# One layer's expert-routing head in another order of work (Trainium2, one core)

## The reference, cut to what matters

```python
x = x + gt1 * (mix @ w_out)
h2 = _rmsnorm(x, n2) * (1 + sc2) + sh2
# _peer(h2):
q = (hf @ wq).reshape(n, PEER_HEADS, 2, PEER_QUERY_DIM // 2)
s = jnp.einsum('nhpd,hpkd->nhpk', q, subkeys)
sv, si = lax.top_k(s, PEER_TOPK)                 # 16 of 128 keys, per half and head
cand = sv[:, :, 0, :, None] + sv[:, :, 1, None, :]
top_v, top_pos = lax.top_k(cand, PEER_TOPK)      # 16 experts per head
gates = jax.nn.softmax(top_v, axis=-1)
act = gelu(einsum('td,tkd->tk', xb, u[eb]))
y = einsum('tk,tkd->td', gb * act, v[eb])
```

## Time and profile before

| | us |
|---|---|
| median of 3 runs | 4270.94 (4268.42 to 4283.64) |
| the profiled execution, own time | 4267.19 |
| its span, first to last instruction | 4265.4 |
| PE busy | 3870.5 (91%) |
| DVE busy | 2707.2 (63%) |
| POOL busy | 1624.6 (38%) |
| ACT busy | 688.1 (16%) |

### The profile page before, as it was taken

How to read it: one execution, slowest core, us unless ns; L and a number is a source line. 1 busy time by engine, 2 the same in 40 slices (tenths; PEclk the granted TensorE clock), 3 DMA queues, 4 the chain that set the end, 5 groups by cost and what they waited for, 6 DMA issues and landing times. The chain is left out here.

```text
span 4265.4 us, 40162 instructions
## 1 busy us (share of the span) xinstructions
PE 3870.5 (91%) x13798; PEld 2277.4 (53%) x13798; DVE 2707.2 (63%) x6039; ACT 688.1 (16%) x1538; POOL 1624.6 (38%) x1498
## 2 busy tenths in 40 slices
PE   1699878889999999999879998688999999999997
PEld 1467657655555555554335675666555555555543
DVE  5855278996666666767522732989876565565443
ACT  1031225530000000000011312455100000000000
POOL 0020005545655654545401100355376565454330
PEclk9896789999999999999989859899999999999998
DMA  6400202368999999999830111133799999999874
GB/s 224 137 14 28 109 15 104 141 221 308 380 381 373 377 370 387 366 382 372 325 137 2 41 40 74 50 126 146 256 389 402 400 361 358 368 349 348 334 277 147
DMA packets 359004, 1025.92 MB, mean 241 GB/s; under 512 B 30225, under 2 KB 131857, under 8 KB 355089
## 3 DMA queue, kind: packets, MB, share of 16 engines
q0 software_dynamic: 147456, 536.94, 32.9%
q1 hardware_dynamic: 205810, 428.62, 27.8%
q10 hardware_dynamic: 5536, 57.80, 3.3%
HBM read 964.02 MB, written 59.22 MB: 240 GB/s over the span
## 5 line engine op out<-in xcount | busy, mean ns | idle before, releaser
L1726 PE MATMUL ps<-colsT,arena 128*128 128x384 f32 x4096 | 1364.3, 487 | 9.5 <-DMA arena<-in_peer_ut 9.5
L1726 PEld LDWEIGHTS ps<-colsT,arena 128*128 128x128 f32 x4096 | 777.3, 191 | 588.1 <-issue 98.5
L1761 PE MATMUL ps<-arena 128*128 128x512 f32 x1536 | 676.5, 592 | 0.0
L1261 POOL DMA_INDIRECT proj<-in_peer_u,eidx x336 | 446.3, 1328 | 255.4 <-DVE modbc L1448 130.5
L1247 POOL TENSOR_SCALAR x<-iota,modbc 128x128 f32<-128x128 f32 x192 | 156.1, 829 | 930.7 <-ACT modbc L1576 787.3
L1261 POOL DMA_INDIRECT proj<-in_peer_v,eidx x335 | 360.7, 1077 | 344.1 <-DVE colsT L1459 243.5
L1761 PEld LDWEIGHTS ps<-arena 128*128 128x128 f32 x1536 | 291.7, 190 | 345.5 <-issue 317.7
L1448 DVE CUSTOM_DVE_ANT_0 proj<-proj,rows 128x1024 f32<-128x1024 f32 x336 | 401.3, 1222 | 77.2 <-DMA proj<-in_peer_u,eidx 75.8
L1459 DVE SCALAR_TENSOR_TENSOR colsT<-proj,modbc,colsT 128x1024 f32<-128x1024 f32 x330 | 409.0, 1285 | 4.2 <-DMA proj<-in_peer_v,eidx 4.1
L1761 PE MATMUL ps<-arena,rows 128*128 128x512 f32 x768 | 344.7, 601 | 13.9 <-DMA arena<-in_peer_v 13.9
L1761 PE MATMUL ps<-arena,x 128*128 128x512 f32 x768 | 341.6, 597 | 7.2 <-DMA arena<-in_peer_v 7.2
(11 more groups left out here) (284 smaller groups left out, 4307.4 us busy)
## 6 DMA issues: line engine op xcount, KB each, us to landing
arena<-in_peer_ut SPq DMA_DIRECT2D x256, 512.0 KB, 7.0
arena<-in_peer_v SPq DMA_DIRECT2D x256, 512.0 KB, 7.0
gmat_d<-arena ACTq DMA_DIRECT2D x24, 2048.0 KB, 6.5
arena<-gmat_d SPq DMA_DIRECT2D x64, 768.0 KB, 18.1
modbc<-in_w_adaT SPq DMA_DIRECT2D x48, 512.0 KB, 4.1
proj<-in_w_adaT SPq DMA_DIRECT2D x48, 512.0 KB, 9.1
arena<-in_w_out SPq DMA_DIRECT2D x2, 4096.0 KB, 14.2
arena<-in_w_q SPq DMA_DIRECT2D x2, 4096.0 KB, 20.8
```

Of the source, the lines that this page charges most:

```text
L1261: pool.indirect_dma_start(ring[slots[at]], None, tab, bass.IndirectOffsetOnAxis(ap=eidx[:, b * SLOTS + q:b * SLOTS + q + 1], axis=0)).then ...
L1726: mm = pe.matmul(ps[:, 2 + j % 2, 0:ND], utab[:, j % UR, k], hT[:, k, NG:T], start=(k == 0), stop=(k == KT - 1))
L1761: mm = pe.matmul(ps[:, Y_BANKS[2 * d + c2], :], wT[j % CR][:, d * P:(d + 1) * P], vtab[:, j % VR, c2 * 512:(c2 + 1) * 512], start=(j == 0) ...
```

## The change

All of it is in the head, in both layers. The amount of arithmetic is the same.

- Query units 0 to 5 are now one block and four heads each: 0 and 1 block 2, 2 and 3 block 3, 4 and 5 block 4. PE does the queries and scores of block 2 before the rows of block 3 are turned.
- The third and fourth output projection are made in halves with other PE work between; PSUM banks change (OP_BANKS, TR_BANKS).
- On ACT the root is a call of its own after the square.
- On DVE, residual, mean and normalisation of the blocks stand at other steps of `route(0)`; those of block 1 (i = 4) move into k = 1: mean after step 0, normalisation after step 1.
- Queries 4 and 5, which stood before the loop over k, are fillers of k = 1; query 9 moves to k = 2; the scores of blocks 4, 0 and 1 stand at (1, 3), (2, 1) and (2, 6).
- The 18 u slices: none in k = 1, 7 in k = 2, 11 in k = 3.
- The turned indices (ijgT) lie in another free row of modbc, and the indirect loads' ring takes its slots in an order that fits this.

```diff
-        QUNITS = ([(2, 2, 2 * i, 2, i) for i in range(4)] + [(4, 1, 4 * i, 4, 2 + i) for i in range(2)]
-                  + [(0, 2, 2 * i, 2, 2 + i % 2) for i in range(4)])
-        TR_BANKS = (4, 6, 2, 2, 2)
+        QUNITS = [(b, 1, 4 * i, 4, 2 + i) for b in DB for i in range(2)] + [(0, 2, 2 * i, 2, 2 + i % 2) for i in range(4)]
+        OP_BANKS = (0, 2, 0, 0, 2)
+        TR_BANKS = (4, 2, 2, 2, 2)
...
-        ijgT = region(modbc, 6 * D, 2, 3, P)
+        ijgT = region(modbc, 2 * D, 2, 3, P)
...
-        G_U = {1: (6, 7), 2: range(G_STEPS), 3: range(G_STEPS)}
-        U_HEAD, U_AHEAD = 18, CR - 1
+        G_U = {1: (), 2: (2, 3, 4, 5, 6, 7, 7), 3: (0, 1, 2, 2, 3, 4, 4, 5, 6, 7, 7)}
+        SCORES_AT = [(1, 3), (2, 1), (2, 6)]
+        U_HEAD, U_AHEAD = sum(len(v) for v in G_U.values()), CR - 1
...
 VectorE:
                 for step in range(STEPS):
                     route(0, step)
+                    if step == 1:
+                        residual(2)
                     if step == 2:
-                        residual(2)
+                        mean(2)
                     if step == 3:
-                        mean(2)
-                    if step == 4:
                         normed(2)
+                    if step == 7:
                         residual(3)
-                    if step == 5:
+                    if step == 8:
                         mean(3)
-                    if step == 6:
-                        normed(3)
-                    if step == 7:
-                        residual(4)
-                    if step == 8:
-                        mean(4)
-                normed(4)
+                normed(3)
+                residual(4)
                 for k in range(1, HEAD_K + 1):
                     for step in range(STEPS):
                         route(k, step)
                         if step < G_STEPS:
                             scatter_rows(k - 1, step)
+                        if k == 1 and step == 0:
+                            mean(4)
+                        if k == 1 and step == 1:
+                            normed(4)
...
 ScalarE:
+                def root(i):
+                    b = WO[i]
                     act.wait_ge(ms_made, i + 1)
...
-                            act.wait_ge(xn_ready, NB)
+                            act.wait_ge(xn_ready, 4)
...
+                def filler_out(k, step):
+                    if (k, step) == (1, 0):
+                        square(4)
+                    elif (k, step) == (1, 1):
+                        root(4)
+                        query_out(4)
+                    elif (k, step) == (1, 2):
+                        query_out(5)
+                    elif k == 1 and step < 5:
+                        turned_rows(step)
+                    elif k == 1:
+                        query_out(1 + step)
+                    elif (k, step) == (2, 0):
+                        query_out(9)
 
                 square(0)
+                root(0)
                 turned_rows(0)
                 square(1)
+                root(1)
+                query_out(0)
+                query_out(1)
+                scores_out(0)
                 turned_rows(1)
-                for u in range(4):
-                    query_out(u)
-                scores_out(0)
+                square(2)
+                root(2)
+                query_out(2)
+                query_out(3)
                 scores_out(1)
-                square(2)
+                turned_rows(2)
                 square(3)
-                turned_rows(2)
-                query_out(4)
-                square(4)
                 exps(0)
-                query_out(5)
+                root(3)
...
 TensorE:
                 out_proj(0)
                 out_proj(1)
                 turn_rows(0)
+                out_proj(2, (0,))
+                query(0)
+                query(1)
+                scores(0)
                 turn_rows(1)
-                for u in range(4):
-                    query(u)
-                scores(0)
-                out_proj(2)
-                out_proj(3)
+                out_proj(2, (1,))
+                query(2)
+                query(3)
                 scores(1)
+                out_proj(3, (0,))
+                turn_rows(2)
+                out_proj(3, (1,))
                 out_proj(4)
-                turn_rows(2)
-                query(4)
-                query(5)
-                scores(2)
                 j = 0
                 for k in range(1, HEAD_K + 1):
                     turn(k - 1)
                     for step in range(G_STEPS):
                         place(k - 1, step)
-                        if k == 1 and step < 6:
-                            filler(step)
-                        if step == 6:
-                            scores(k + 2)
-                        if step in G_U[k]:
+                        filler(k, step)
+                        if (k, step) in SCORES_AT:
+                            scores(SCORES_AT.index((k, step)) + 2)
+                        for _ in range(G_U[k].count(step)):
                             u_stage(j)
                             j += 1
```

More of the change, by code:

```diff
@@ L1112, in build @@
         x_again = region(arena, 8192, len(DB), D)
-        ring = [region(proj, q * D, D) for q in range(5)] + [modbc[:, q:q + D] for q in (2 * D, 5 * D, D)]
+        ring = [region(proj, q * D, D) for q in range(5)] + [modbc[:, q:q + D] for q in (5 * D, 2 * D, D)]
         EARLY = len(ring)
@@ L1254, in _ @@
                     tab = tab_u if kind == "u" else tab_v
-                    if at == EARLY - 1:
+                    if at == EARLY - 2:
                         pool.wait_ge(g_mm, ND // 4)
@@ L1275, in residual @@
                     dve.wait_ge(wo_mm, i + 1)
-                    bank = 2 * (i % 2)
+                    bank = OP_BANKS[i]
                     c.link(dve.tensor_tensor(rb[:, b], ps[:, bank:bank + 2, :].rearrange("p a n -> p (a n)"), mb[:, v, G1], ALU.mult))
@@ L1635, in _ @@
                         spread(k - 1, step)
-                        if k == 1 and step < 6:
-                            filler_out(step)
+                        filler_out(k, step)
                         if step == 3:
                             scores_out(k + 1)
-                        if step in G_U[k]:
+                        for _ in range(G_U[k].count(step)):
                             gelu(j)
@@ L1658, in _, with out_proj @@
             def _(pe):
-                def out_proj(i):
+                def out_proj(i, halves=(0, 1)):
                     b = WO[i]
                     if i in (2, 3):
-                        pe.wait_ge(q_out, 2 * (i - 1))
+                        pe.wait_ge(x_ready, 2 * i - 3)
                     if i == 4:
-                        pe.wait_ge(x_ready, 3)
-                    for n in range(2):
+                        pe.wait_ge(hT_ready, HT_COUNT[2])
+                    for n in halves:
                         for k in range(KT):
-                            mm = pe.matmul(ps[:, 2 * (i % 2) + n, :], mixT[:, k, b * P:(b + 1) * P],
+                            mm = pe.matmul(ps[:, OP_BANKS[i] + n, :], mixT[:, k, b * P:(b + 1) * P],
                                            w_out[:, k, n * 512:(n + 1) * 512], start=(k == 0), stop=(k == KT - 1))
-                    mm.then_inc(wo_mm, 1)
+                    if 1 in halves:
+                        mm.then_inc(wo_mm, 1)
                 def turn_rows(i):
@@ L1673, in turn_rows @@
                     pe.wait_ge(xn_ready, i + 1)
[L1674 to L1677, removed]
                     if i == 4:
                         pe.wait_ge(hT_ready, HT_COUNT[3])
+                    elif i >= 1:
+                        pe.wait_ge(q_out, 2 * i)
                     for k in range(KT):
@@ L1688, in query @@
                         pe.wait_ge(wq_landed, 16)
-                    pe.wait_ge(hT_ready, HT_COUNT[1 if u < 4 else 2 if u < 6 else 4])
-                    if u < 4:
-                        pe.wait_ge(x_ready, 1 + u // 2)
+                    pe.wait_ge(hT_ready, HT_COUNT[u // 2 if u < 6 else 4])
+                    if u < 2:
+                        pe.wait_ge(x_ready, 2)
+                    if u == 4:
+                        pe.wait_ge(x_ready, NB)
                     if u >= 8:
@@ L1704, in scores @@
                     b = ORDER[k]
-                    pe.wait_ge(q_out, (4, 4, 6, NQ, NQ)[k])
+                    pe.wait_ge(q_out, (2, 4, 6, NQ, NQ)[k])
                     if k == 0:
@@ L1734, in turn @@
                     else:
-                        pe.wait_ge(x_ready, NB)
+                        pe.wait_ge(x_ready, 4)
                     pe.transpose(ps[:, 0, 0:P], ijF[:, 0], ident[:, :])
@@ L1763, in v_stage, with filler @@
                     mm.then_inc(vt_mm, 1)
[L1765 to L1769, removed]
+                def filler(k, step):
+                    if k == 1 and 1 <= step < 3:
+                        query(3 + step)
```

(6 more changed lines are left out.)

## The result

The changed kernel takes 4242.45 us (median of 4 runs, 4233.95 to 4245.32) against 4270.41 before (median of 4 runs, one more than in the table before): 28.0 us less, 0.65%. The ratio on record is 0.9921, 95% interval 0.9902 to 0.9941, so 0.79%; the interval holds both figures. The forecast was 4239.4, a gain of 0.74%. Its profiled execution took 4241.51 us, with a span of 4239.7. PE is still busy for 91% of the span, and in the first loop it is nearly as full as before, 1058.43 of 1069.90 us.

What follows compares the result with a forecast made beforehand. PE's own work bounds the loop, so it must begin earlier; 22.9 + 18.1 − 4.3 − 20.95 = 15.75 us a layer, 31.5 off 4267.19 gives 4235.7, plus 3.75 for the median: 4239.4; range 4220 to 4264.

Steps and rivals of the forecast that it cites:

- first scores: Head's start: DVE's first routing starts at 521.5 instead of 544.37, −22.9 us a layer.
- k = 0: Routing of block 2: waits of 14.85 and 1.19 go, a root wait of 1.3 comes; −18.1 us a layer.
- k = 1: Second routing: 9.4 us of `place` waits go, block 1's work and two 6.6 us waits come; +4.3 us a layer.
- start of k = 2 to the 18th slice: PE paces k = 2 and 3; two more slices, query 9 and one scores add 20.95 us a layer.
- behind it, to the first v slice: Behind the head: the 5.07 us stall for a u slice stays, change 0, ends −5 and +5.
- rival 1: The 9.4 us of `place` waits in k = 1 stay; gain 6.3 a layer or 1.3; 4258 to 4268; chance 0.24.
- The exponentials' wait: In k = 2 and 3, waits for the exponentials behind two slices might lengthen, 5 us more.
- rival 2: 6 us absorbed in k = 2 and 3 and the 5.07 stall gone; gain 26 a layer, 4219; chance 0.12.
- Rival 3: PE's clock drops in k = 1; half clock for share 0.51 costs the whole gain, 0.7 gives 4302; chance 0.10.
- The table loads: A root's two ACT table loads take 1.28 us each; the skill's 2.66 would cost 5.5 us more a layer, 4250.

Runs made afterwards that it cites:

- a3: Rows of blocks 2 and 3 turned and their four query units made before the first scores again, against the changed kernel; 4292.61 us, ratio 1.0057.
- a1: Block 1's mean and normalisation each one step later in k = 1 than in the changed kernel; 4215.36 us, ratio 0.9881 to the kernel before.
- b1: On top of a1, turnings and query units 6 to 9 placed in k = 1, two scores one step earlier in k = 2; 4214.84 us, ratio 0.9868.
- a4: Against the changed kernel, k = 3 gets 8 u slices instead of 11, three more follow behind the head; 4244.81 us, ratio 0.9945.
- c2: On top of b2, one u slice moved from the end of k = 2 to the end of k = 3; 4198.30 us, ratio 0.9829.
- b2: On top of a1, SP loads the second and third gate group and v slice four u slices later; 4196.71 us, ratio 0.9815.
- b3: On top of a1, POOL's first indirect load waits until 24 u slices are done; 4201.72 us, ratio 0.9826.
- c3: On top of b2, only query 9 moves on PE, from step 0 of k = 2 to the end of k = 1; 4194.85 us, ratio 0.9814.

## Why the prediction was right, point by point

| term, us a layer | forecast | layer 0 | layer 1 |
|---|---|---|---|
| first scores | −22.9 | −19.8 | −23.5 |
| k = 0 | −18.1 | −18.0 | −17.6 |
| k = 1 | +4.3 | +6.3 | +5.2 |
| start of k = 2 to the 18th slice | +20.95 | +21.0 | +20.5 |
| behind it, to the first v slice | 0 | +0.4 | +2.7 |
| sum | −15.75 | −10.2 | −12.8 |

The forecast of 31.5 us met 28.0 in the medians, of which the heads hold 22.9. The total is nearer than the sum of its terms, and that is luck: 2.8 us came from outside the heads, which the forecast did not treat, and 2.3 from the spread between the profiled executions and the medians.

- **First scores.** The steps were right: the queries' end to DVE's start is again 6.24 us (523.53 less 517.29). What is missing in layer 0 is the first two projections, 30.60 us instead of the 27.70 that I took from one row. Windows at the head's start, the kernel before and then the changed one, both in layer 0:

```profile
465.70:473.00 7.30, 7.28 (x17) 3.33 (x18) 0.00 (x0) 0.00 (x0) 0.00 (x0) 1.00 0.85 323
```

```profile
464.60:472.00 7.40, 7.34 (x11) 3.18 (x12) 0.00 (x0) 0.00 (x0) 0.00 (x0) 0.60 0.86 317
```

  PE stood still 1.61 us ahead of both, and both came from the same instructions of the mixer at a granted clock of 0.50 (all of 435.00 to 460.00 in the changed kernel, 436.00 to 460.50 before). In the kernel before the clock was up before the projection began, in the changed kernel only within it. The 5 us ahead of each start, in the same order:

```profile
460.70:465.70 5.00, 3.03 (x22) 2.60 (x22) 1.25 (x6) 1.43 (x4) 0.00 (x0) 0.93 0.00 0
```

```profile
459.70:464.70 5.00, 3.16 (x15) 2.60 (x15) 1.11 (x5) 1.43 (x4) 0.00 (x0) 0.50 0.00 0
```

  The kernel before had its own slow start in layer 1 (0.56 in the first 7 us, 30.73 for the projections). So about 3 us of this term belong to the execution and not to the kernel. The query unit measured 7.2, near the 7.07 chosen between 6.7 and 8.5.
- **k = 0.** The waits of 14.85 and 1.19 went, the new one is 1.39 (forecast 1.3), and the projections stayed ahead of DVE. a3 shows the cover's edge: with the front undone k = 0 grows by 4.5.
- **k = 1.** The waits were foreseen at 6.6 each and measured 6.4 and 8.3. The mis-sized term is the second: `spread` of step 1 ended 617.86 − 608.87 = 9.0 us after the scatter's start, not 8.2, since PE had stood still for 8.63 us and did the first sixteen `place` instructions in 3.75 us, where before each eight of that step took 1.13; root came 0.4 later, and the scatter that covers took 4.18 instead of 4.6. a1 shows that both are on the path. The 9.4 us of waits for `place` did go (0.7 left); rival 1 is refuted, and b1 shows how little room there was.
- **k = 2 and 3.** The count of moved PE work, 20.95, met 21.0 and 20.5. a4 and c2 show why: slices change sides without a change in time. The exponentials' wait of 5.3 us was named as a possible 5 us and cost nothing. The 6 us that rival 2 expected to be absorbed here were not.
- **Behind the head.** I kept the stall as it was. It went from 5.07 to 5.62 and from 4.39 to 5.67. That is 1.3 of the 2.7 us in layer 1, where the granted clock of the stage also fell from 0.97 to 0.95. My reason was incomplete: besides the landing, SP's own issue of the load came 3.7 us late behind a v load. b2 and b3 show that it could have been lost whole, for 8.8 us.
- **Rival 3** was half there: the granted clock of k = 1 fell from 0.92 to 0.86, f of about 0.28, below the 0.51 at which the gain would have been gone.
- **The table loads.** From `mean(4)`'s side the root is again four instructions back to back, 618.27 to 621.28, 3.0 us; and the new wait of k = 0 is 1.39 us. The Trainium skill ("ScalarE: Activation LUTs", What ACT_TABLE_LOAD costs) adds a drain of about 1.4 us to every switch to another set; in these 3.0 us there is no place for it.

## What to carry to other kernels

When a chain of stages is bound first by one engine and then by another, cut it at fixed marks and count each stage by the engine that paces it: a wait removed where its engine paces is worth its length (14.4 of 14.7 us in a1), and one removed where another engine paces is worth nothing (5.3 us in c2). Work that waits for a second engine's answer should be asked for a step after that engine can have it; here one step later shortened k = 1 by 14.4 and 14.1 us in the two layers, about as much as the whole change had gained in the medians (28.0). Where a mark sits on one engine, check where the others are at that moment before a gain or a loss is read from it (c3).

## What the runs showed of the hardware

The same code, behind the same instructions and the same idle of 1.61 us, began once at a granted clock of 1.00 and once at the lower level, worth 2.9 us in 30. It is not the order of the kernel's work: of the 24 head starts in the twelve profiles 11 had 1.00 in their first 7 us and 13 a mean of 0.56 to 0.65, and two layers of one execution could differ.

A single load's issue can hold SP's queue for 7.97 us, and 1.48 where POOL's first eight indirect loads are not beside it; the next load on that queue, needed sooner, waits behind it. Indirect loads alone do not do this: the median of all 256 issues of v loads in the changed kernel is 0.33 us, most of them in the loops, where indirect loads run too.
